# Compressed attention over one group's 64 keys, with the high and low parts stacked, and new engine orders

## The chip, the cores and the metric

One core of a Trainium2 chip runs the whole program in one launch. The metric is the device time of one execution in microseconds, as the median of several runs.

## The reference, cut to what matters

The reference is one conditioned decoder layer over 1024 tokens of width 1024: a gated feed-forward block, a mixer with two attention groups, a second feed-forward block and a final normalisation. The change lies in the first attention group, which has 8 query heads in 2 groups and three branches. Its compressed branch is this:

```
kc = compress_blocks(k_cmp, ...); vc = compress_blocks(v_cmp, ...)   # 63 blocks of each group, head size 64
s = einsum('bqgrd,bcgd->bgrqc', qb, kc) * scale
p_cmp = masked_softmax(s, cmp_end[None, :] <= t[:, None])
o_cmp = einsum('bgrqc,bcgd->bqgrd', p_cmp, vc)
o = g0 * o_cmp + g1 * o_slc + g2 * o_win
```

The other branches attend to all past keys (16 blocks of 64 are selected out of 16, so that all visible ones are taken) and to a window of 512 keys. The second attention group is a causal attention with a forgetting term, called FoX.

## The kernel before, in words

The first feed-forward block comes first, then the mixer's projections (126 products on TensorE, `mix`), then attention, the output projections and the second feed-forward block. All operands of large products are split into a high and a low part in the type fp32r, so that a product is two or three matmuls.

Attention is cut into 64 units (`A_UNITS`). A unit of the first group, kind N, is one of 2 groups g, one of 8 tiles i of 128 queries, and one of the three branches br: compressed (CMP), selected (SLC), window (WIN). It has 4 rows, one for each head of the group. The last 16 units are FoX. A row's scores are 128 queries by 128 keys times `A_LEN`; a compressed row has length 1, that is 128 keys, of which 64 belong to the group g and 64 to the other group; the mask closes those of the other group. The 244 key blocks of 128 (`A_BLOCKS`, 148 of them in the N units, 16 of these compressed) are what the value products run over.

Each unit passes through the engines so. On TensorE `scores` puts the mask in PSUM by a matmul with an identity in bf16 and then adds two matmuls for each row (high keys, low keys). On VectorE `row_max` (M) reads the scores from PSUM; on ScalarE `exp` (E) reads them too and writes the weights and their sum to SBUF; VectorE takes the reciprocal (R); on GpSimd `scale` (C) multiplies by it and by the branch's gate. TensorE transposes a block of 4 rows (T, `transpose_block`) into one of two PSUM banks; ScalarE copies that rounded as the high part (H, `high`); VectorE subtracts for the low part (L, `low_part`); TensorE multiplies both with the values (V, `values`) and accumulates over all blocks of the units of one g and i. Then the halves of a sum are added (U on ScalarE and A on VectorE), split (G, O) and stored.

Each engine does its operations in the order of a string written out in the file: `A_PE` (S scores, T, V, U for a later product), `A_DVE`, `A_ACT`, `A_POOL`. The k-th letter of a kind is its k-th item. An engine waits at an operation whose input is not there, with all behind it. T of block b waits for L of block b-2 (two PSUM banks), H of b for V of b-3 (three buffers `pt`). Scores use four PSUM banks; a pack of scores waits until the rows last in its bank have been read by E.

The masks are made once by GpSimd (`attention_masks`) at step 50 of the mixer's projections.

Of the kernel before, what the change touches and what calls it, by code (L numbers as in the profile page):

```python
# [17 lines left out]
F32 = mybir.dt.float32  # L18
# [7 lines left out]
P = 128  # L26
# [53 lines left out]
A_SUMS = [(4 * u + r, max(k, 2)) for u, r, k in A_PACKS if k > 1 or r % 2 == 0]  # L80
A_SUM_OF = [n for n, (_, k) in enumerate(A_SUMS) for _ in range(k)]
# [65 lines left out]
A_DVE = ("LMMRMLMRMRRLMMRRMLMALLRLLMMMMLMRRRMMMMRRALLMMLMLMMLMRRRRLMLRMARMLLMLRMLMLRMLLMLRMLMRLLALMMLRLMLMLRMLRMLLMLRMLMRLMALMLLMR"  # L147
         "LMRLMLRMLLMLRMLMLRLLMMRALLMLLMRLMLRMLLMLRMMRMRMMRMMRRMLMRRLMMRLMALRLMLLLLLRMLRMLMMRMRMMMRMLMLMMLMRMRRMRLLALRLALLMLMRLMLM"
         "RLALMLLMRLMLRMLMRLALMLLMLRMLLMRLMLMRLMALLMRLLMLRLLMMRLLMLMLRALMLMLLRLLMMRLLMLRMLMLRMLMARLLMLLLLRMLLMLMMRMLMLMRLRALMLMLRM"
         "LMMLLLRLLMMLMRRLMLMLRMLMMRLLMMRALMLMLRALMLLMLLMMRRLMMLMLLRRMALMLMLLRALLLLMMRLLMMLLMRRALMLMLLALRLLMLMMRLLMMLLMRRALMLMLLAL"  # L150
         "RLLMLMMRLLMMLLMRRALMLMLLMLRALLMMRLLMMLMLLMRRALMLMLLRALLLRLLLALLLLALLLLLLLLALLLLALLLLLLA")
A_ACT = ("EHEEEEHEEEEEEEHEEEEHEEEUHHGEEHHEEEHEEEEEEEEEUHHGEHEHEEHEEEHEEEHEEUEHHGEHEHEHEHHEHEHEEEEHEHUHGHEHEHEHEHEHHEHEHEEEEHUEHEHG"
         "HEHEHEHEHHEHEHEEEEHEHHUEHHGEHHEHEHEHHEHEEEEEEEEEEEEEEEEEEEHEEEEHEEEHUEHEEHGHHHHEHEHEEHEEEEEEEEEHEEHEEHEEEEEHHUEHEGHUHEHG"
         "HEHEHEHUHEGHHEHEHEHEEEEHUHGEHHEHEHHEHEHEHUEHHGEHEHEEEHEHHEHHEHUHEHEGHHHEEHHEHHEEEEHEHEHEHUEHHGHHHEHEHHEHEEHEEHEHUHEGHEHE"
         "HHHHEHHEEHEEHEHEHEHEHHUEEHEEHUGHEHEGHHEHHEEHEHEEHHUEHEGHUHHHGHEHHEHHEEHUHEEHEGHUHHHEHHGEHEHHEEUHHEEHEGHUHHHEHHGEHEHHEEUH"
         "HEEHEGHUEHHHEHHGEHHEEHEEHHUEHEGHUHHHEHHGEHHHUHHGHHUHGHHHHHHHUHHGHHUHGHHHHHUG")
# [191 lines left out]
def build(nc, aps, outs):  # L348
    ctx = ExitStack()
    with ctx:  # L350
# [157 lines left out]
        kc_hi = sb("kc_hi", [P, P], F32R)  # L508
        kc_lo = sb("kc_lo", [P, P], F32R)
# [12 lines left out]
        cmp_mask, far_edge, causal, ident_b = masks[:, 0:2048], masks[:, 2048:2176], masks[:, 2176:2304], masks[:, 2304:2432]  # L522
        edges = masks[:, 2048:2304]
# [101 lines left out]
        def s_ps(s):  # L625

            p = A_PACK_OF[s]
            u, r, k = A_PACKS[p]
            n, bank = A_LEN[u][r], A_BANK[p]
            at = bank * HALF + (s % 4 - r) * n * P + (P if n == 5 else 0)  # L630
            return at, at + n * P
# [514 lines left out]
        def _(act):  # L1146
# [480 lines left out]
            def exp(s):  # L1627

                act.wait_ge(asem["mx"], A_PACK_OF[s] + 1)
# [3 lines left out]
                act.activation(p_at(s), ps_flat[:, lo:hi], ACT.Exp, bias=negmax[:, col(s)], accum_out=rowsum[:, col(s)]).then_inc(asem["ex"], 1)  # L1633

            def high(b):

                c = a_first_row(b) * P
# [3 lines left out]
                act.copy(pt[b % 3][:, c:HALF], ps[:, 5 - b % 2, c:HALF]).then_inc(asem["ph"], 1)  # L1641
# [234 lines left out]
        def _(pool):  # L1876
# [102 lines left out]
            def attention_masks():  # L1979
# [3 lines left out]
                own(1, pool.memset(cmp_mask, NEG))  # L1983
# [112 lines left out]
        def _(dve):  # L2096
# [685 lines left out]
            def mix():  # L2782
# [3 lines left out]
                for g in range(3, M_PROD + 7):  # L2786
# [3 lines left out]
                    if g == M_PROD - 2:  # L2790
                        row_max(0)
# [903 lines left out]
```

## Time and profile before

| | us |
|---|---|
| median of 3 runs (2257.72 to 2258.95) | 2257.76 |
| the profiled execution, its own time | 2259.06 |
| its span, first to last instruction | 2257.3 |
| TensorE busy (PE) | 2218.7, 98% |
| VectorE busy (DVE) | 1560.2, 69% |
| ScalarE busy (ACT) | 1074.1, 48% |
| GpSimd busy (POOL) | 909.2, 40% |

PE is TensorE's matmuls, PEld its weight loads, which overlap matmuls. Matmuls are pipelined and overlap too, so that the cost of one in a stream is the distance between two starts, not its duration. Attention lies between 1063 and 1442 us of the span, its compressed units between 1063 and 1305 us.

### The profile page before, as it was taken

To read this page: it belongs to the slowest core of one execution; us is meant where nothing else is said; L and a number is where in the kernel's file an instruction comes from. 1 tells how busy PE (TensorE), PEld (TensorE's weight loads), DVE (VectorE), ACT (ScalarE), POOL (GpSimd) and SP (SyncE) were. 2 spreads that over 40 slices of the span, in tenths; PEclk is the share of its full clock that TensorE was granted. 3 is DMA by queue.
4 is the path that set the end of the run, shared out by engine and by line. 5 is a ranking of instruction groups with operands and counts; after the bars stand their busy time and mean duration, and the time that the engine had idled before them with its cause. 6 is when DMAs were issued, how large, how long until landed. Compare 5 with 4: busy or idle time off the path is not lost. (4 is left out here: it accounts for less than half of the span.)

```text
span 2257.3 us, 29610 instructions
## 1 busy us (share of the span) xinstructions
PE 2218.7 (98%) x10552; PEld 1821.8 (81%) x10552; DVE 1560.2 (69%) x2100; ACT 1074.1 (48%) x2026; POOL 909.2 (40%) x784
## 2 busy tenths in 40 slices
PE   7999999999999999999999999999999999999998
PEld 6888888888878888888787877788778888888887
DVE  7966767488869657632888889568786454547765
ACT  5533333333545543433989888424443333333344
POOL 0045555400123555543767555446305555530013
PEclk9999999999999999999999999999999999999999
DMA  7155665374661533454714056324223232347454
GB/s 283 70 203 213 212 220 208 133 285 154 205 224 39 173 98 143 168 187 127 196 43 113 20 124 171 110 93 159 103 74 118 98 112 95 108 156 271 142 180 159
DMA packets 152034, 338.02 MB, mean 150 GB/s; under 512 B 14224, under 2 KB 36880, under 8 KB 151888
## 3 DMA queue, kind: packets, MB, share of 16 engines
q1 hardware_dynamic: 150624, 333.57, 43.7%
q10 hardware_dynamic: 1264, 2.56, 0.5%
q8 instruction: 85, 1.39, 0.3%
q14 instruction: 61, 0.50, 0.1%
HBM read 247.28 MB, written 86.64 MB: 148 GB/s over the span
## 5 line engine op out<-in xcount | busy, mean ns | idle before, releaser
L3132 PE MATMUL ps<-r_main,r_z 128*128 128x512 f32 x1232 | 482.3, 391 | 6.5 <-DVE r_main L2176 3.6
L1928 POOL TENSOR_TENSOR r_z<-f_main,r_z 128x512 fp32r<-128x512 f32 x213 | 304.7, 1432 | 446.8 <-ACT r_z L1202 446.8
L3133 PE MATMUL ps<-r_main,r_z 128*128 128x512 f32 x1232 | 480.3, 390 | 0.0
L3134 PE MATMUL ps<-r_main,r_z 128*128 128x512 f32 x1232 | 480.0, 390 | 0.0
L1202 ACT CAST r_z<-f_main 128x512 fp32r<-128x512 f32 x254 | 155.5, 620 | 347.0 <-PE ps L3134 277.7
L3132 PEld LDWEIGHTS ps<-r_main,r_z 128*128 128x128 f32 x1232 | 231.7, 188 | 60.2 <-DVE r_main L2176 4.6
L3134 PEld LDWEIGHTS ps<-r_main,r_z 128*128 128x128 f32 x1232 | 231.8, 188 | 48.9
L3133 PEld LDWEIGHTS ps<-r_main,r_z 128*128 128x128 f32 x1232 | 231.8, 188 | 47.6 <-issue 0.2
L3278 PE MATMUL ps<-r_main 128*128 128x512 f32 x604 | 235.9, 390 | 0.2 <-DVE r_main L2428 0.2
L3280 PE MATMUL ps<-r_main 128*128 128x512 f32 x604 | 235.0, 389 | 0.0
L3279 PE MATMUL ps<-r_main 128*128 128x512 f32 x604 | 235.0, 389 | 0.0
L1964 POOL TENSOR_TENSOR r_z<-f_main,r_z 128x512 fp32r<-128x512 f32 x108 | 153.6, 1436 | 176.7 <-ACT r_z L1422 176.5
L3359 PE MATMUL ps<-r_main,r_z 128*128 128x512 f32 x504 | 198.7, 394 | 1.1 <-DVE r_main L2179 0.5
L3361 PE MATMUL ps<-r_main,r_z 128*128 128x512 f32 x504 | 196.4, 390 | 0.0
L3360 PE MATMUL ps<-r_main,r_z 128*128 128x512 f32 x504 | 196.3, 390 | 0.0
L2845 DVE TENSOR_TENSOR r_main<-ps,r_main 128x512 fp32r<-128x512 f32 x244 | 151.3, 635 | 34.8 <-ACT r_main L1641 31.5
L1641 ACT CAST r_main<-ps 128x512 fp32r<-128x512 f32 x244 | 130.7, 548 | 32.4 <-PE ps L3477 22.9
L3278 PEld LDWEIGHTS ps<-r_main 128*128 128x128 f32 x604 | 113.4, 188 | 24.5 <-issue 1.1
L3279 PEld LDWEIGHTS ps<-r_main 128*128 128x128 f32 x604 | 113.4, 188 | 24.1 <-issue 0.5
L3280 PEld LDWEIGHTS ps<-r_main 128*128 128x128 f32 x604 | 113.4, 188 | 23.4
L2830 DVE TENSOR_REDUCE negmax<-ps 128x1 f32<-128x640 f32 (+7 forms) x160 | 124.2, 790 | 7.1 <-PE ps L3464 4.8
L3359 PEld LDWEIGHTS ps<-r_main,r_z 128*128 128x128 f32 x504 | 94.6, 188 | 23.2 <-issue 2.7
(380 smaller groups left out, 4552.3 us busy)
## 6 DMA issues: line engine op xcount, KB each, us to landing
act_d<-f_main SPq DMA_DIRECT2D x154, 256.0 KB, 2.0
f_main<-act_d SPq DMA_DIRECT2D x70, 512.0 KB, 4.8
f_main<-in_ada SPq DMA_DIRECT2D x56, 512.0 KB, 5.2
f_main<-in_wg SPq DMA_DIRECT2D x20, 1024.0 KB, 5.0
f_main<-in_wu SPq DMA_DIRECT2D x20, 1024.0 KB, 5.0
f_w<-in_wo SPq DMA_DIRECT2D x40, 512.0 KB, 3.9
f_main<-in_wmix SPq DMA_DIRECT2D x18, 1024.0 KB, 5.5
f_e<-in_we SPq DMA_DIRECT2D x10, 1024.0 KB, 5.7
```

The lines of the kernel that those rows point to most:

```text
L1202: act.copy(prod_hi_t[SLOTS[g]], source_of(g)).then_inc(s["wh"], 1)
L1928: pool.tensor_tensor(prod_lo_t[slot], source_of(g), prod_hi_t[slot].bitcast(F32), ALU.subtract).then_inc(s["wl"], 1)
L1964: pool.tensor_tensor(m_lo[g % M_RING], mix_source(g), m_hi[g % M_RING].bitcast(F32), ALU.subtract).then_inc(s["wl"], 1)
L3132: pe.matmul(out, wh, hi, start=start, stop=False, skip_group_check=True)
L3133: pe.matmul(out, wh, lo, start=False, stop=False, skip_group_check=True)
L3134: return pe.matmul(out, wl, hi, start=False, stop=stop, skip_group_check=True)
L3278: pe.matmul(out, wh, hi, start=k == 0 and j in (1, 7, 2), stop=False, skip_group_check=True)
L3279: pe.matmul(out, wh, lo, start=False, stop=False, skip_group_check=True)
L3280: pe.matmul(out, wl, hi, start=False, stop=k == PAIRS - 1, skip_group_check=True).then_inc(fsem[f]["dn"], 1)
L3359: pe.matmul(out, wh, hi[:, k], start=q in (1, 7) and k == 0, stop=False, skip_group_check=True)
L3360: pe.matmul(out, wh, lo[:, k], start=False, stop=False, skip_group_check=True)
L3361: mm = pe.matmul(out, wl, hi[:, k], start=False, stop=k == 3, skip_group_check=True)
```

## The change

Scores of a compressed unit are taken over the group's own 64 keys alone. High and low keys lie side by side (`kc_st`), so that one matmul of 2 times 64 columns for each row takes the place of two of 128, and the two halves are not added in PSUM: a new VectorE operation D (`score_sum`) adds them and writes 64 sums a row to SBUF. The row maximum and the exponential read these. Weights of a compressed row are 64 columns; the transposed block has 64 partitions; its high part goes to partitions 0 to 63 and its low part to partitions 64 to 127 of the same columns. The values of a group stand twice on the partitions (`vc_twice`), and one matmul takes the place of two. The masks are smaller and made by fewer operations, and two GpSimd copies and two ScalarE copies (step 90 of the mixer's projections) make `vc_twice`. A pack of scores that follows a compressed one in its bank waits for D instead of E. All four order strings are new, for FoX too, with a D for each compressed unit but the first, whose D is in the mixer's stage.

```diff
+A_CMPS = [p for p, (u, _, _) in enumerate(A_PACKS) if A_UNITS[u][3] == CMP]
...
+def a_cols(s):
+    return HD if A_UNITS[s // 4][3] == CMP else a_len(s) * P
...
-A_PE = ("TSSTSSVSTSSVTSSVTTVTVTSSVSTSSVSSSSVVTTSSTVTSVSTSTSVTSVVVSVTTSSTVTSVTSVTSVTSVTTSVTSVTVVTSSTVTVVSTVTSVTSVTSVTSVTTSVTSVTSVTV"
-        "SVTSVTTSVVTSVTSVTSVTTSVTSVTVVTSSTTVVVSTVTSVTVTSVTSVTSVTTSSTSSSSSVSSVTSSVTSVVTVSTVTVTVTVTVTSVTSSTSSTSSSVSSVSTSVTSSTSVVVTVT"
-        "VTVTVSTSTVVTSTSVVTSVTVTSVTTSVTSVTSVTVSTVVTVSTVTSVTSVTTSVTSVTSVTVSTVTVSTVTVVTSSTTVVVSTVTSVTVSTVSTVTVTVTSSTTVVSVTTSVTSVTSVT"
-        "SVTVSVTVTVTVTVTSVTSVTTSSVTSSVSTVVTSTVSTVVTSTSSVVTVTVTVTSSVTTSVVTSSTVVTSTSSVVTVSSTTSVVSTVTVSTVTSVTVTSSVTTSSVTSVVTVSTTSVVST"
-        "VTVTVTVTVTVSSTTVSSTVVTSVTTSVVSTVTVTVTVTSTVTVSSTVSSVTVTSVTTSVVSTVTVTVTVTSTVTVSSTVSSVTVTSVTTSVVSTVTSVTTVVTSSVTVTVSTSTSVVTSV"
-        "TTSVVSTVTVTVTVTVTVTVTVTVTVUTTVVUTVTVUTVTVTVUTVTTVVUTVTVUTTVVUTVTVUTVTVTVTVVV")
-A_DVE = ("LMMRMLMRMRRLMMRRMLMALLRLLMMMMLMRRRMMMMRRALLMMLMLMMLMRRRRLMLRMARMLLMLRMLMLRMLLMLRMLMRLLALMMLRLMLMLRMLRMLLMLRMLMRLMALMLLMR"
...
+A_PE = ("SSTSSTSVTSTVSSVTTSSVTTSSSVVSTVSVSTTVSTSSSSVSTSTVVSVTTSVVSTTVSTSVTSVTSVTSVTSVSTVTSVTVTVTSSTVVVSTSVTTSVTSVTSVTSVVTTSVVTTSV"
+        "TTSVTSVVVSTTSVTSVTSVSTVTSVTTVVVTSTSVVTVSTTSVVTSTSVTSVTSVTSSSVVTSTSVTSSVTSVVTTSVSTTVSVTSVVTSSSVSSTTSSVTVTSSVSTSTVSSVTSTVV"
+        "STVTTVVTSSTVVTSVTSVVTTSVSTVTSVSTVTVSTTVSTVVTVSVTTSVTSVTVSTVTSVTSVTVTSVTSVTTVVTSSTVVTVSVTTSVVTTVSTVTSVTSVTSVTVTSVTSVTTSVT"
+        "SVVVTSVTTSVTTVVVTSVTTSVTSVSVTSSTSVTVTSVVTTSVTVTSVTTSSVVVTSTSVSTTSVVSTTSVVTSSVTVVTSTSVTSVTSVTTSVVTSVTTVVSSTTVSSTVSVTSVTVS"
+        "TVSTTVVTVTVTVTSSVTVVTSSTVTSVTTSVVSTTVVTVVTTSVTVTSSVTSSVVTTSVTTSVVSTTVVTVVTTSTVTVSSTVSSVVTTSVTVVSTTSVTSVTTVVTVSSTVTSVTSVS"
+        "TVTSVTVSTVSTTVVTVVTTVTVTVVTUTVVTTUVVTTUVTVTUVTVTUVTVTTVVUTVVTTVTVUTVTVTVTUVTVTVVV")
+A_DVE = ("DMRMMMRLMLDRRLMMRLRMLLMMRAMMRLMMRLDLRMALMMRRMMLMMLMMLRLRDMLRMLRMALMLMLMLMRLRMLRMLDRRMLLMLLMLMALMRLRMRLMLMRLMLLDRMLLMLLML"
...
+A_EARLY = [("D", 0), ("M", 0), ("M", 1), ("M", 2)]
+A_MX = {e: n + 1 for n, e in enumerate(A_EARLY + [e for e in stages(A_DVE, D=1, M=3) if e[0] in "DM"])}
...
-        kc_hi = sb("kc_hi", [P, P], F32R)
-        kc_lo = sb("kc_lo", [P, P], F32R)
+        kc_st = sb("kc_st", [P, 2, P], F32R)
+        kc_hi, kc_lo = kc_st[:, 0], kc_st[:, 1]
...
-        cmp_mask, far_edge, causal, ident_b = masks[:, 0:2048], masks[:, 2048:2176], masks[:, 2176:2304], masks[:, 2304:2432]
-        edges = masks[:, 2048:2304]
+        cmp_mask, far_edge, causal, ident_b = masks[:, 0:512], masks[:, 512:640], masks[:, 640:768], masks[:, 768:896]
+        edges = masks[:, 512:768]
+        cmp_sums = ft(19, 2)[:, 6 * P:10 * P].rearrange("p (a r c) -> p a r c", a=2, r=4)
+        vc_twice = rt(33)[:, 4 * P:6 * P].rearrange("p (g m) -> p g m", g=2)
...
+            at = A_BANK[p] * HALF + (s % 4 - r) * n * P + (P if n == 5 else 0)
+            return at, at + a_cols(s)
...
-            return p_space[seg][:, pos:pos + a_len(s) * P]
+            return p_space[seg][:, pos:pos + a_cols(s)]
+
+        def compressed_scores(u):
+
+            lo = s_ps(4 * u)[0]
+            return ps_flat[:, lo:lo + HALF].rearrange("p (r k c) -> p r k c", r=4, k=2)
+
+        def summed(u):
+
+            return cmp_sums[:, u // 3 % 2]
+
+        def compressed_block(b):
+
+            return A_UNITS[A_BLOCKS[b][0]][3] == CMP
+
+        def block_cols(b):
+
+            return slice(a_first_row(b) * P, HALF)
...
+                    if g == 90:
+                        act.wait_ge(s_mask, 8)
+                        for k in range(2):
+                            to, source = slice((1 - k) * HD, (2 - k) * HD), slice(k * HD, (k + 1) * HD)
+                            act.copy(vc_twice[to, k], vc_st[source].bitcast(F32)).then_inc(s_mask, 1)
...
-                act.wait_ge(asem["mx"], A_PACK_OF[s] + 1)
+                act.wait_ge(asem["mx"], A_MX["M", A_PACK_OF[s]])
                 if A_PLACE_FREED[s] is not None:
                     act.wait_ge(asem["tr"], A_PLACE_FREED[s] + 1)
                 lo, hi = s_ps(s)
-                act.activation(p_at(s), ps_flat[:, lo:hi], ACT.Exp, bias=negmax[:, col(s)], accum_out=rowsum[:, col(s)]).then_inc(asem["ex"], 1)
+                scored = summed(s // 4)[:, s % 4] if A_UNITS[s // 4][3] == CMP else ps_flat[:, lo:hi]
+                act.activation(p_at(s), scored, ACT.Exp, bias=negmax[:, col(s)], accum_out=rowsum[:, col(s)]).then_inc(asem["ex"], 1)
 
             def high(b):
 
-                c = a_first_row(b) * P
+                c = block_cols(b)
                 act.wait_ge(asem["tr"], b + 1)
                 if b >= 3:
                     act.wait_ge(asem["pv"], b - 2)
-                act.copy(pt[b % 3][:, c:HALF], ps[:, 5 - b % 2, c:HALF]).then_inc(asem["ph"], 1)
+                keys = HD if compressed_block(b) else P
+                act.copy(pt[b % 3][0:keys, c], ps[0:keys, 5 - b % 2, c]).then_inc(asem["ph"], 1)
...
+                pool.wait_ge(q_["cmp"], chain("cl", 1))
+                own(1, pool.memset(masks[:, 0:768], 0.0))
+                steps = cmp_mask.rearrange("p (i c) -> p i c", i=NT)
+                own(2, pool.affine_select(out=steps, in_=steps, compare_op=ALU.is_ge, fill=NEG, base=-31,
+                                          pattern=[[P, NT], [-16, HD]], channel_multiplier=1))
...
+                    own(7 + g, pool.tensor_copy(vc_twice[rows, g], vc_st[rows].bitcast(F32)))
...
+                        score_sum(0)
...
+            def score_sum(p):
+
+                rows = compressed_scores(A_PACKS[p][0])
+                dve.wait_ge(asem["sd"], p + 1)
+                dve.tensor_reduce(summed(A_PACKS[p][0]), rows.rearrange("p r k c -> p r c k"), AX.X, ALU.add).then_inc(asem["mx"], 1)
+
             def row_max(p):
 
                 u, r, k = A_PACKS[p]
                 s = 4 * u + r
                 lo, hi = s_ps(s)
+                if A_UNITS[u][3] == CMP:
+                    dve.wait_ge(asem["mx"], A_MX["D", A_CMPS.index(p)])
+                    dve.tensor_reduce(negmax[:, col(s, k)], summed(u), AX.X, ALU.max, negate=True).then_inc(asem["mx"], 1)
+                    return
...
+                if compressed_block(b):
+                    dve.tensor_tensor(pt[b % 3][HD:P, c], ps[0:HD, 5 - b % 2, c], pt[b % 3][0:HD, c].bitcast(F32), ALU.subtract).then_inc(asem["pl"], 1)
...
-                        pe.wait_ge(s_mask, 9)
+                        pe.wait_ge(s_mask, 10)
...
-                if A_BANK_FREED[p] is not None:
-                    pe.wait_ge(asem["ex"], A_BANK_FREED[p] + 1)
+                freed = A_BANK_FREED[p]
+                if freed is not None and A_UNITS[freed // 4][3] == CMP:
+                    pe.wait_ge(asem["mx"], A_MX["D", A_CMPS.index(A_PACK_OF[freed])])
+                elif freed is not None:
+                    pe.wait_ge(asem["ex"], freed + 1)
...
-                    mask = cmp_mask[:, g * T + i * P:g * T + (i + 1) * P]
-                else:
-                    mask = causal
+                    pe.matmul(compressed_scores(u)[:, :, 0], ident_b, cmp_mask[:, i * HD:(i + 1) * HD].unsqueeze(1).to_broadcast([P, 4, HD]),
+                              start=True, stop=False, skip_group_check=True)
+                    for r in range(4):
+                        mm = pe.matmul(compressed_scores(u)[:, r], q_n[g][r][:, i * P:(i + 1) * P], kc_st[:, :, g * HD:(g + 1) * HD],
+                                       start=False, stop=True, skip_group_check=True)
+                    mm.then_inc(asem["sd"], 1)
+                    return
...
+                keys = HD if compressed_block(b) else P
                 for r in range(a_first_row(b), 4):
-                    mm = pe.transpose(ps[:, 5 - b % 2, r * P:(r + 1) * P], p_at(4 * u + r)[:, j * P:(j + 1) * P], ident_f[:])
+                    mm = pe.transpose(ps[0:keys, 5 - b % 2, r * P:(r + 1) * P], p_at(4 * u + r)[:, j * P:j * P + keys], ident_f[:])
...
-                elif br == CMP:
-                    v = vc_st[:]
-                else:
+                elif br != CMP:
                     if i == 0 and br == SLC:
                         pe.wait_ge(s_nv[g], 32)
...
+                if br == CMP:
+                    mm = pe.matmul(ps[:, 6 + og % 2], vc_twice[:, g], pt[b % 3][:, 0:HALF], start=True, stop=False, skip_group_check=True)
+                    mm.then_inc(asem["pv"], 1)
+                    return
                 out = ps[:, 6 + og % 2, c:HALF]
-                pe.matmul(out, v, pt[b % 3][:, c:HALF], start=b == A_START[og], stop=False)
-                pe.matmul(out, v, pt[b % 3][:, HALF + c:T], start=False, stop=b == A_LAST[og]).then_inc(asem["pv"], 1)
+                pe.matmul(out, v, pt[b % 3][:, c:HALF], start=b == A_START[og], stop=False, skip_group_check=kind == "N")
+                pe.matmul(out, v, pt[b % 3][:, HALF + c:T], start=False, stop=b == A_LAST[og], skip_group_check=kind == "N").then_inc(asem["pv"], 1)
```

## Rows read from the trace of the kernel before

**Rows 1.** The page's first part, busy time and share of each engine.

```profile
PE 2218.7 (98%) x10552; PEld 1821.8 (81%) x10552; DVE 1560.2 (69%) x2100; ACT 1074.1 (48%) x2026; POOL 909.2 (40%) x784
```

**Rows 2.** Stretches: length, busy us (instructions) of PE PEld DVE ACT POOL, clock, DMA.

```profile
1062.90:1180.00 117.10, 112.27 (x730) 93.89 (x729) 95.80 (x172) 98.72 (x274) 71.11 (x102) 1.00 0.50 133
1180.00:1225.00 45.00, 42.25 (x273) 33.37 (x273) 36.90 (x76) 41.26 (x135) 37.11 (x61) 1.00 0.48 117
1225.00:1310.00 85.00, 84.58 (x538) 68.74 (x537) 73.58 (x122) 73.03 (x164) 44.80 (x54) 1.00 0.12 30
1310.00:1442.00 132.00, 126.39 (x786) 100.14 (x785) 109.37 (x209) 109.72 (x254) 66.73 (x76) 1.00 0.55 145
```

**Rows 3.** The same: the start, two slices of short units, one of FoX.

```profile
1062.90:1119.00 56.10, 52.23 (x340) 42.94 (x339) 42.97 (x87) 47.27 (x151) 36.07 (x61) 1.00 0.83 221
...
1080.00:1100.00 20.00, 18.53 (x116) 13.98 (x116) 17.01 (x36) 19.32 (x62) 15.86 (x28) 1.00 1.03 267
...
1200.00:1220.00 20.00, 18.33 (x114) 13.76 (x113) 16.48 (x35) 18.93 (x58) 14.84 (x24) 1.00 0.93 225
...
1360.00:1380.00 20.00, 19.00 (x122) 14.88 (x119) 18.31 (x36) 17.72 (x42) 11.77 (x15) 1.00 0.81 230
```

**Rows 4.** TensorE in order of time around one compressed unit's scores and values.

```profile
1118.98 0.38 PE L3444 MATMUL ps<-f_z 128*128 128x512 bf16 x1
1119.01 0.41 PE L3463 MATMUL ps<-kc_hi,r_main 128*128 128x128 f32 x1
1119.26 0.28 PE L3464 MATMUL ps<-kc_lo,r_main 128*128 128x128 f32 x1
...
1119.93 0.27 PE L3464 MATMUL ps<-kc_lo,r_main 128*128 128x128 f32 x1
1120.04 0.45 PE L3500 MATMUL ps<-r_main 128*128 128x512 f32 x1
...
1121.57 0.28 PE L3463 MATMUL ps<-r_main 128*128 128x256 f32 x1
1121.69 0.28 PE L3464 MATMUL ps<-r_main 128*128 128x256 f32 x1
1121.81 0.40 PE L3500 MATMUL ps<-r_main 128*128 128x512 f32 x1
...
1123.18 0.40 PE L3500 MATMUL ps<-r_main,vc_st 128*128 128x512 f32 x1
1123.42 0.39 PE L3501 MATMUL ps<-r_main,vc_st 128*128 128x512 f32 x1
```

**Rows 5.** Matmuls that read `kc_hi` (four a unit), by stretches.

```profile
1062.00:1100.00 38.00, 4.32 (x16) 3.09 (x16) 0.00 (x0) 0.00 (x0) 1.00 0.98 259
1100.00:1180.00 80.00, 5.40 (x20) 3.83 (x20) 0.00 (x0) 0.00 (x0) 1.00 0.28 74
1180.00:1225.00 45.00, 4.32 (x16) 3.11 (x16) 0.00 (x0) 0.00 (x0) 1.00 0.48 117
1225.00:1310.00 85.00, 3.24 (x12) 2.32 (x12) 0.00 (x0) 0.00 (x0) 1.00 0.12 30
```

**Rows 6.** Groups of VectorE by shape, whole span: reductions.

```profile
L2830 DVE TENSOR_REDUCE negmax<-ps 128x1 f32<-128x256 f32 x8 | 3.3, 417 | 0.2
...
L2833 DVE TENSOR_REDUCE negmax<-ps 128x2 f32<-128x512 f32 x8 | 5.5, 681 | 1.2 <-PE ps L3464 1.2
```

**Rows 7.** Groups of ScalarE by shape: exponentials, and copies from PSUM and SBUF.

```profile
L1633 ACT ACTIVATE f_main<-ps,negmax 128x640 f32<-128x640 f32 x27 | 21.6, 801 | 3.7 <-DVE negmax L2830 3.6
L1633 ACT ACTIVATE f_main<-ps,negmax 128x128 f32<-128x128 f32 x59 | 21.3, 385 | 4.4 <-DVE negmax L2833 4.2
...
L1527 ACT ACTIVATE hid_f<-hid_f 128x128 f32<-128x128 f32 x2 | 0.6, 310 | 0.0
L1525 ACT COPY hid_a<-ps 128x128 f32<-128x128 f32 x2 | 0.5, 264 | 0.0
```

**Rows 8.** The mixer's stage when GpSimd makes the masks (steps around 50).

```profile
830.00:860.00 30.00, 30.00 (x135) 24.80 (x134) 22.48 (x31) 10.03 (x19) 21.84 (x21) 1.00 0.30 106
```

**Rows 9.** Waits in 1310 to 1442 us: engine, tile, line, releaser: sum, times, longest.

```profile
PEld ps L3477 <- DVE r_main L2845: 15.3, 32, 0.9
DVE r_main L2845 <- ACT r_main L1641: 14.8, 29, 1.4
```

More of the change, by code:

```diff
@@ L152 @@
[L152 to L156, printed above, removed]
@@ L628, in s_ps @@
             u, r, k = A_PACKS[p]
-            n, bank = A_LEN[u][r], A_BANK[p]
-            at = bank * HALF + (s % 4 - r) * n * P + (P if n == 5 else 0)
-            return at, at + n * P
+            n = A_LEN[u][r]
+            at = A_BANK[p] * HALF + (s % 4 - r) * n * P + (P if n == 5 else 0)
+            return at, at + a_cols(s)
         ps_flat = ps[:].rearrange("p a b -> p (a b)")
@@ L1982, in attention_masks @@
                 pool.wait_ge(m_["pair"], 128)
-                own(1, pool.memset(cmp_mask, NEG))
-                own(2, pool.memset(masks[:, 2048:2304], 0.0))
-                for g in range(2):
-                    m = cmp_mask.rearrange("p (g i e c) -> p g i e c", g=2, i=NT, e=2)[:, g, :, g, :]
-                    own(3 + 2 * g, pool.memset(m, 0.0))
-                    own(4 + 2 * g, pool.affine_select(out=m, in_=m, compare_op=ALU.is_ge, fill=NEG, base=-31,
-                                                      pattern=[[P, NT], [-16, HD]], channel_multiplier=1))
@@ L1991, in attention_masks @@
-                own(7, pool.affine_select(out=causal, in_=causal, compare_op=ALU.is_ge, fill=NEG, base=0,
-                                          pattern=[[-1, P]], channel_multiplier=1))
-                own(8, pool.affine_select(out=far_edge, in_=far_edge, compare_op=ALU.is_ge, fill=NEG, base=-1,
-                                          pattern=[[1, P]], channel_multiplier=-1))
-                own(9, pool.tensor_copy(ident_b, ident_f[:]))
-                pool.wait_ge(q_["gt"], 1)
-                own(10, pool.affine_select(out=gate_t[:, 0, 0:24:3], in_=gate_t[:, 0, 0:24:3], compare_op=ALU.is_ge, fill=0.0, base=-31,
-                                           pattern=[[0, 8]], channel_multiplier=1))
+                pool.wait_ge(q_["cmp"], chain("cl", 1))
@@ new lines, in attention_masks @@
+                own(1, pool.memset(masks[:, 0:768], 0.0))
+                steps = cmp_mask.rearrange("p (i c) -> p i c", i=NT)
+                own(2, pool.affine_select(out=steps, in_=steps, compare_op=ALU.is_ge, fill=NEG, base=-31,
+                                          pattern=[[P, NT], [-16, HD]], channel_multiplier=1))
+                own(3, pool.affine_select(out=causal, in_=causal, compare_op=ALU.is_ge, fill=NEG, base=0,
+                                          pattern=[[-1, P]], channel_multiplier=1))
@@ new lines, in attention_masks @@
+                own(4, pool.affine_select(out=far_edge, in_=far_edge, compare_op=ALU.is_ge, fill=NEG, base=-1,
+                                          pattern=[[1, P]], channel_multiplier=-1))
+                own(5, pool.tensor_copy(ident_b, ident_f[:]))
+                pool.wait_ge(q_["gt"], 1)
+                own(6, pool.affine_select(out=gate_t[:, 0, 0:24:3], in_=gate_t[:, 0, 0:24:3], compare_op=ALU.is_ge, fill=0.0, base=-31,
+                                          pattern=[[0, 8]], channel_multiplier=1))
@@ L2001, in _ @@
+                for g in range(2):
+                    rows = slice(g * HD, (g + 1) * HD)
+                    own(7 + g, pool.tensor_copy(vc_twice[rows, g], vc_st[rows].bitcast(F32)))
             for g in range(M_PROD):
@@ L2841, in low_part @@
             def low_part(b):
[L2843 removed]
+                c = block_cols(b)
                 dve.wait_ge(asem["ph"], b + 1)
[L2845 to L2846 removed]
+                if compressed_block(b):
+                    dve.tensor_tensor(pt[b % 3][HD:P, c], ps[0:HD, 5 - b % 2, c], pt[b % 3][0:HD, c].bitcast(F32), ALU.subtract).then_inc(asem["pl"], 1)
+                else:
+                    dve.tensor_tensor(pt[b % 3][:, HALF + c.start:T], ps[:, 5 - b % 2, c], pt[b % 3][:, c].bitcast(F32),
+                                      ALU.subtract).then_inc(asem["pl"], 1)
             def o_add(og):
@@ L2856, in _ @@
             dve.wait_ge(s_mask, 10)
-            for kind, k in stages(A_DVE, M=3, R=2):
-                if kind == "M":
+            for kind, k in stages(A_DVE, D=1, M=3, R=2):
+                if kind == "D":
+                    score_sum(A_CMPS[k])
+                elif kind == "M":
                     row_max(k)
@@ L3449, in scores @@
                         q = q2 = q_n[g][r][:, i * P:(i + 1) * P]
-                        k1, k2 = (kc_hi, kc_lo) if br == CMP else (k1_n[g][br], k2_n[g][br])
-                        key0 = 0 if br == CMP else (i + 1 - n) * P
+                        k1, k2 = k1_n[g][br], k2_n[g][br]
+                        key0 = (i + 1 - n) * P
                     else:
```

23 lines of the change are left out of this document (13 added, 10 removed).

## The prediction

> **What bounds the kernel now.** I read the page's busy shares first. TensorE is busy for 98% of the span and VectorE for 69% [rows 1]; this is a kernel bound by TensorE, and a change is worth what it takes from TensorE's stream or from TensorE's waits. The change only touches attention, 1063 to 1442 us, so I read that next, by stretches [rows 2]. The reader should see four different places. In 1225 to 1310 TensorE sits idle for 0.4 of 85 us: every nanosecond of its stream counts. In 1063 to 1180 it is idle for 4.8 of 117.1, 3.9 of it before 1119 [rows 3]. In 1180 to 1225, where the second group begins with its short units, it is idle for 2.75 of 45 us. FoX has 5.6 idle of 132. The granted clock is 1.00 in all of them, the 2.4 GHz level, and TensorE was hardly ever idle before, so I expect no change of clock. The slices of short units show who limits there: ScalarE has 19.3 and 18.9 of 20 us in them [rows 3]. In FoX it is the ring T, H, L that shows: transposes wait 15.3 us for VectorE's low part, and that waits 14.8 us for ScalarE's high part [rows 9] (TensorE's weight loads run ahead, so of the 15.3 only part is lost). VectorE's share in the tight stretches is 82% (95.8 of 117.1) and 87% (73.6 of 85) [rows 2], its highest slice 92% [rows 3].
>
> **TensorE's stream, one compressed unit.** From the mask's start at 1118.98 to the start of what follows the scores at 1120.04 is 1.06 us [rows 4]. It is made of mask and first matmul, 0.28 (to 1119.26), and seven more steps of 0.111. After the change there are one mask matmul of 256 columns and four matmuls of 128. Two matmuls of 256 columns in a row start 0.12 apart, and two of 512 start 0.24 apart (1123.18 to 1123.42) [rows 4], so 256 columns fewer in the mask are worth some 0.11; the first pair is 0.17, three more steps 0.33, together 0.50 to 0.51. Saved: 0.55 us. The values go from two matmuls of 512 columns to one: 0.235 us saved, between the 0.24 just read and the 0.23 that such pairs take elsewhere. The four transposes keep their 128 moving columns but have 64 stationary columns instead of 128. A step is 0.11 us at 128 moving columns and 0.12 at 256 [rows 4], so at 128 it is not the moving columns that set it; it could be the weight load, which the change halves, or a cost of each instruction, which it doesn't. No row has 64 stationary columns. Bounds: nothing, or down to the pace of the moving columns, 0.12/2 = 0.06, which is 0.2 us for four. I take the middle, 0.1.
>
> The Trainium skill (TensorE: Matmul & The Clock Gate, section "LDWEIGHTS (loading the stationary operand)") says that a load takes its number of columns over 1.2, in ns: 107 ns for 128, 53 for 64. That fits the 0.11 of a step, and by it the four transposes would save 0.2 us a unit, 3.2 us over 16 units in place of my 1.6. No trace here shows a load of 64 columns.
>
> **Where that counts.** Scores of the 16 units fall 4, 5, 4 and 3 into 1062 to 1100, 1100 to 1180, 1180 to 1225 and 1225 to 1310 (four matmuls with `kc_hi` a unit) [rows 5]; value products follow some microseconds later, by the same order 3, 4, 3 and 6. In the second and the fourth stretch TensorE hardly waits: 8 scores by 0.55 is 4.4, and 10 value blocks by 0.235 + 0.1 is 3.35, together 7.75 us. The first unit's scores stand inside the mixer's products, where TensorE never stops: 0.55. In the short units 7 scores and 6 value blocks would be 3.85 + 2.0 = 5.85; there ScalarE or the way through C is late next, and I take half, 2.9 (bounds: none, all). Sum 11.2; if all counted, 14.15.
>
> **VectorE.** A unit gains D, a reduction that reads 512 scores a partition, and M reads 256 sums instead of 512 scores. D: the nearest row is a reduction of 512 elements, 0.68 us; M: 0.42 at 256 elements [rows 6]. So D and M are 1.10 where M was 0.68: 0.42 more, 6.7 us over 16 units. D reads its pairs 64 columns apart and writes 256 results instead of 2; no row has that. Below: 0.68. Above: twice it, 1.36, if each written result cost as much as a read one, which would be 10.9 us more in all. I take 0.68, since the same line costs the same for 2 results and for 1. In 1225 to 1310 VectorE would go from 73.6 to 74.8 us (three D) while TensorE's stretch shrinks from 85 by 3 x 0.55 + 6 x 0.335 = 3.7 to 81.3: a share of 92%, that of its highest slice now [rows 3]. It gets no cover beyond that, and I charge 1.2 us for it (bounds: 0; and 5, worked out below).
>
> **ScalarE.** 64 exponentials go from 128 to 64 columns. From 640 to 128 columns the duration falls from 801 to 385 ns, 0.81 a column, so 52 ns each [rows 7], 3.3 us in all. But they now read SBUF instead of PSUM, and the two operations on the hidden layer, both of 128 columns, are 310 ns from SBUF and 264 from PSUM [rows 7]. With those 46 ns the saving is 6 ns each, 0.4 us in all: I take nothing. So the ScalarE-bound slices don't get shorter by this.
>
> The Trainium skill (VectorE: DVE Perf Modes, section "The TRN2 errata — SBUF-src ops pay a fixed extra latency per instruction") speaks against the change here: ScalarE's fixed cost is 224 cycles from SBUF and 172 from PSUM, 43 ns more. The trace's 46 ns agrees. By columns alone ScalarE would save 3.3 us, by the rule 0.6.
>
> H and L keep their 512 columns, with half the partitions, and cost the same: a pass goes by columns. The extra two ScalarE copies (about 0.3 each, from the 310 ns row) are hidden, as ScalarE is busy for a third of the mixer's stage (10 of 30 us in this slice) [rows 8].
>
> **GpSimd and the masks.** The mask work gets smaller (a clearing of 768 in place of 2048 and more) and moves behind one more wait. It happens where GpSimd is busy for 22 of 30 us while TensorE is busy for all 30 [rows 8]; the scores that need it come 74 products later. Nothing on the path, and if that cover were gone some 2 us. `scale` for compressed rows gets shorter by some 50 ns each, which helps only in the short units.
>
> **Orders and waits.** The new D adds 0.68 us to the way from scores to exponential and M gives 0.26 back; a row's scores are issued several blocks ahead of its transposes, so this is covered except in the first two or three units of a group. What the wait for D replaces (for E of all four rows) comes earlier, in TensorE's favour. In the two strings I counted how many letters of TensorE lie between T and V of a block: the mean falls from 8.1 to 7.0 (8.7 to 7.3 in the N units), and pairs 4 or fewer apart rise from 3 to 13. That is room for H and L given away; on the other side the few very long ones (16 to 20) are gone. I take 0 for both and keep 3 us each way.
>
> **Sum.** -11.2 + 1.2 = -10.0 us. Against the profiled execution's own 2259.06 (its span 2257.3 and 1.8 around it) that is 2249.1; against the median of the runs, 2257.76, which is 1.3 below, 2247.8. I give the latter. Its own range is 2243 to 2251.
>
> **Rivals.**
> More: all of 14.15, transposes at 0.2 instead of 0.1 (1.6 more), no loss to VectorE, and the orders save some of the 13.6 us that TensorE now idles, say a fifth: about -17, 2240 to 2243. For it: idle is concentrated in a few places [rows 2], and the earlier release of the bank. Against: those places are limited by ScalarE, which saves nothing.
>
> VectorE becomes the bound: if it can't pass a share of 88% where it is now 87%, the 74.8 us of 1225 to 1310 need 85.0, and that stretch gains nothing; in 1100 to 1180, where its share is lower, the gain stays. That takes 3.7 away from 10 and leaves -6.3. If D takes 1.36 us as well, eight of them in the two tight stretches ask for 8 x 0.68 / 0.88 = 6.2 us more, and nothing is left of the gain. Between the two, nearer to the first: -5, 2253. For it: FoX, where VectorE's slices reach 92%, has TensorE at 95% [rows 3]. Against: at 87% TensorE lost just 0.5% of its time.
>
> Nothing measurable comes of it: the two together with an order that is worse by 3 to 5 us; 2254 to 2262.
>
> Slower: T and V closer together. The way T, H, L is about 0.6 + 0.6 + 0.7 = 2 us; one letter of TensorE is 379/681 = 0.56 us, so 4 letters (2.2 us) just cover it and 7 leave 1.9 us for H and L to queue behind E and M. If that queueing is as long as the room, every missing letter costs. It decides from 14.5 us on, 0.06 us for each of the 244 blocks; at 0.1 us a block it is +24 - 10 = +14, 2272; at 0.075, +8, 2266. For it: the waits of T for L and L for H in FoX. Against: the mean room of 1.9 us.
>
> **Chances.** My forecast 0.48, more 0.16, VectorE the bound 0.17, nothing 0.12, slower 0.07. About 0.2% (4.5 us) can be told from no change in this kernel. Faster is the first two and most of the third, at 2253.2 and below: 0.78; same 0.15; slower 0.07. The range 2240 to 2255 leaves out the far end of "more" and most of the last two.
>
> **What would show it.** In the profile after: a compressed unit's scores 0.5 us from the mask to the next product, and one values matmul; transposes of compressed blocks 0.06 to 0.11 apart; a D of 0.68 and an M of 0.4; exponentials of 64 columns near 380 ns; 1225 to 1310 shorter by 3 to 4 us with TensorE idle under 1 us. A TensorE that waits more for L in the N units, or D at 1 us or above, would make the forecast wrong; so would FoX differing by over 3 us, as only its order changes.

## The result and the profile after

The changed kernel takes 2237.99 us (median of 4 runs, 2237.17 to 2239.31) against 2257.74 of before beside it. The ratio is 0.9912, 95% interval 0.9900 to 0.9925: 19.8 us less (17 to 23). The forecast was 10.0 less, with 2240 as its lower end. The profiled span is 2236.3 us, 21.0 below that of before.

The page's first part after answers to [rows 1]:

```profile
PE 2201.5 (98%) x10472; PEld 1811.9 (81%) x10472; DVE 1560.2 (70%) x2116; ACT 1071.6 (48%) x2028; POOL 904.3 (40%) x782
```

Eighty matmuls are gone, 64 of the scores and 16 of the values. VectorE has just the busy time of before, though by durations D adds 10.9 us and the shorter M's give back 4.4; what made up the rest isn't shown (run 1 below, with the same operations, has 1564.7).

TensorE's instructions by line after: masks of the compressed scores, their values, and the last matmul of the other blocks' values (duration in ns least/median/most, first and last start).

```profile
L3493 PE MATMUL ps<-f_z x16: 272/283/286, 1062.9 to 1259.8; 128*128 128x256 bf16 x16
...
L3558 PE MATMUL ps<-r_main,r_z x16: 391/408/501, 1076.8 to 1287.9; 128*128 128x512 f32 x16
...
L3563 PE MATMUL ps<-r_main x228: 273/393/404, 1078.9 to 1419.5; 128*128 128x512 f32 x98, 128*128 128x256 f32 x16
```

The same work before (scores of the high keys in place of the masks):

```profile
L3463 PE MATMUL ps<-kc_hi,r_main x64: 272/277/412, 1063.1 to 1275.4; 128*128 128x128 f32 x64
...
L3501 PE MATMUL ps<-r_main x228: 272/395/403, 1080.7 to 1439.7; 128*128 128x512 f32 x98, 128*128 128x256 f32 x16
...
L3501 PE MATMUL ps<-r_main,vc_st x16: 388/394/401, 1077.4 to 1304.8; 128*128 128x512 f32 x16
```

Attention begins within 0.2 us of where it began. The last compressed value product comes 16.9 us earlier and attention's last product 20.2 us. So the time was won inside attention. The last matmul of the 148th values product, the N units' last, starts 17.5 us earlier (1325.7 before, 1308.2 after), and 2.7 us more are won behind it, in FoX. The mixer before attention and all that follows it are the same within 1 us.

Prices after, by shape: D, M of compressed units, their L.

```profile
L2863 DVE TENSOR_REDUCE f_z<-ps 128x256 f32<-128x512 f32 x16 | 10.9, 681 | 0.5 <-PE ps L3496 0.4
...
L2872 DVE TENSOR_REDUCE negmax<-f_z 128x4 f32<-128x256 f32 x16 | 6.6, 415 | 0.3
...
L2892 DVE TENSOR_TENSOR r_main<-ps,r_main 64x512 fp32r<-64x512 f32 x16 | 11.0, 685 | 1.3 <-ACT r_main L1676 0.7
```

TensorE around one compressed unit:

```profile
1077.55 0.27 PE L3493 MATMUL ps<-f_z 128*128 128x256 bf16 x1
1077.58 0.64 PE L3496 MATMUL ps<-kc_st,r_main 128*128 128x128 f32 x4
1078.19 0.60 PE L3537 MATMUL ps<-ident_f,f_main 128*64 128x128 f32 x4
1078.54 0.48 PE L3562 MATMUL ps<-r_main 128*128 128x512 f32 x1
```

Four transposes with 64 stationary columns (1078.19) take 0.35 us to the next start. Scores with their mask take 0.64 us here (1077.55 to 1078.19), and less elsewhere, as 0.52 at 1062.93 to 1063.45. D and M cost what the rows of before said, to 2 ns. TensorE's stream is 0.55 + 0.235 us shorter a unit, 12.6 in all. That leaves 7 us and more of the 19.8 which no shorter instruction of TensorE explains, and in the forecast only 11.2 of the stream was to count.

What did change is how long TensorE waits. Waits before, 1225 to 1310 us (the stretch of which I had said that every nanosecond counts), and after, 1212 to 1293, which holds about the same blocks: engine, tile, line, releaser, sum, times, longest.

```profile
DVE r_main L2845 <- ACT r_main L1641: 7.1, 17, 1.1
PEld ps L3477 <- DVE r_main L2845: 4.3, 14, 0.5
```

```profile
PEld ps L3537 <- DVE r_main L2894: 1.7, 7, 0.5
```

The weight loads of transposes (PEld) waited 14 times for a low part, 4.3 us in all, in a stretch in which TensorE had counted as busy for 84.58 of 85 us [rows 2]; after, 7 times and 1.7 us. Low parts waited 7.1 us for ScalarE's high parts, and 2.3 after.

### The profile page after: what moved, and what is told of

The parts are those of the page before. It is cut to its first block, busy times and chain, and to the rows that moved or that the text cites. A ratio compares the mean times of both kernels' runs of the same rounds, so it can differ in the third digit from the quotient of the medians.

```text
span 2236.3 us, 29463 instructions
## 1 busy us (share of the span) xinstructions
PE 2201.5 (98%) x10472; PEld 1811.9 (81%) x10472; DVE 1560.2 (70%) x2116; ACT 1071.6 (48%) x2028; POOL 904.3 (40%) x782
## 4 chain that ended last, share of the span: by engine, by line
PE 80%; DVE 12%; ACT 3%; issue 2%; DMA 1%; SPq 1%; POOL 1%; DVEq 0%; ACTq 0%; POOLq 0%
PE ps L3183 11%; PE ps L3184 11%; PE ps L3185 11%; PE ps L3331 6%; PE ps L3329 6%; PE ps L3330 6%; PE ps L3410 4%; PE ps L3412 4%; PE ps L3411 4%; PE ps L3537 3%; PE ps L3562 2%; PE ps L3141 2%; PE ps L3142 2%; PE ps L3143 2%; PE ps L3563 1%
## 5 line engine op out<-in xcount | busy, mean ns | idle before, releaser
L2894 DVE TENSOR_TENSOR r_main<-ps,r_main 128x512 fp32r<-128x512 f32 x228 | 141.3, 629 | 27.0 <-ACT r_main L1676 24.5
L1676 ACT CAST r_main<-ps 128x512 fp32r<-128x512 f32 (+1 forms) x244 | 129.1, 544 | 22.8 <-PE ps L3537 18.5
```

## The experiments

Each was timed beside the kernel before, whose median was 2257.7 (2258.1 beside runs 14 and 15). "Gain" is against it. The last column is read from each run's trace: from the first matmul of the first compressed scores to that of the 148th values product, that is, the N units. It was 262.4 us before and 245.0 after. It helps because the place where attention begins moves from execution to execution, 1061.3 to 1064.1 us, whatever the kernel; differences of 1 or 2 us between medians have to be read with that in mind.

| | median us | ratio, 95% interval | N units us |
|---|---|---|---|
| 1 edit, old orders | 2256.04 | 0.9991, 0.9982 to 1.0001 | 261.7 |
| 2 new orders, old computation | 2251.69 | 0.9971, 0.9959 to 0.9983 | 257.5 |
| 3 new orders but old from FoX on | 2239.26 | 0.9918, 0.9903 to 0.9932 | 245.3 |
| 4 D twice | 2243.79 | 0.9937, 0.9922 to 0.9952 | 249.8 |
| 5 short stream, old orders | 2254.35 | 0.9986, 0.9977 to 0.9995 | 258.9 |
| 6 short stream, new orders | 2243.48 | 0.9938, 0.9922 to 0.9955 | 250.4 |
| 7 sums in PSUM, no D | 2246.36 | 0.9949, 0.9934 to 0.9964 | 252.2 |
| 8 values twice | 2240.60 | 0.9925, 0.9910 to 0.9940 | 245.9 |
| 9 bank freed by E | 2240.71 | 0.9929, 0.9912 to 0.9945 | 248.6 |
| 10 before, half of L | 2253.10 | 0.9978, 0.9969 to 0.9987 | 257.0 |
| 11 after, half of L | 2235.49 | 0.9901, 0.9886 to 0.9916 | 242.5 |
| 12 edit, old orders, half of L | 2250.20 | 0.9967, 0.9954 to 0.9980 | 255.8 |
| 13 short stream, old orders, half of L | 2249.70 | 0.9966, 0.9953 to 0.9978 | 253.9 |
| 14 as 13, and half of H | 2241.14 | 0.9925, 0.9911 to 0.9940 | 246.2 |
| 15 as 12, and half of H | 2243.23 | 0.9933, 0.9916 to 0.9949 | 249.3 |
| 16 before, half of H | 2250.69 | 0.9967, 0.9955 to 0.9980 | 255.2 |
| 17 after, half of H | 2235.31 | 0.9900, 0.9885 to 0.9915 | 240.9 |

**1. The edit in the old orders.** The changed kernel with the four old strings; in `A_DVE` a D ahead of each compressed M.

```diff
-A_DVE = ("DMRMMMRLMLDRRLMM...   # and A_PE, A_ACT, A_POOL of the changed kernel
+A_DVE = ("LDMMRMLMRMRRLDMM...   # those of before, with D ahead of M
```

> The edited computation with the order strings of the kernel before; a D stands in VectorE's string right ahead of the M of its compressed pack. Theory A (the edit's TensorE stream gives at most 12.6 us, the other 7 us came from the new orders): 2245 to 2250, a gain of 8 to 12 us over before. Theory B (the edit alone is worth the whole 20 us, by relieving VectorE, ScalarE and the banks too, and the orders matter little): 2237 to 2241. Theory C (the edit needs its orders, since D and the shorter blocks shift every queue): no gain or a loss, 2255 or above.

**2. The new orders alone.** The kernel before with the new strings, D's taken out.

> The kernel before with the four new strings, the D letters taken out; the computation is that of before. Theory A: the new orders gain 5 to 8 us by themselves, 2250 to 2253. Theory B: within 2 us of before. Theory C (orders that fit only the new durations): slower than before, 2260 or above.

**3. The old order from FoX on.** Strings of the changed kernel up to the point, at the end of the N units, where both have issued the same items; the old ones behind it.

> The changed kernel, with the strings of the kernel before from the point on at which the first FoX units begin (both orders have issued the same items up to there). By block counts in the two traces FoX gave 3.7 us of the 20. If that is FoX's own order: 3 to 4.5 us slower than the changed kernel, 2241 to 2242.5. If it is only what the queues carry over from the N units: within 1 us of the changed kernel.

The edit by itself gains 1.7 us (an interval of 0.9982 to 1.0001, so it can hardly be told from nothing), the orders by themselves 6.0, both 19.8. They don't add up: with the new strings the edit is worth 13.7.

Run 3 is 1.3 us slower than the changed kernel, between its two expectations, but in its trace attention also began 1.6 us earlier (1061.4 against 1063.0), which hides a part. From the 145th values product, behind which TensorE's strings part, to attention's last one it takes 119.6 us against 116.5 in the changed kernel and 120.3 before. So of the 3.8 us that this stretch gained, 3.1 are its own order, and 0.7 it took over from the units before.

The trace of run 1 shows where the edit's gain went. In 1225 to 1310 us, once more:

```profile
PEld ps L3537 <- DVE r_main L2894: 6.7, 18, 0.7
```

```profile
1225.00:1310.00 85.00, 82.97 (x520) 66.19 (x518) 75.12 (x125) 71.88 (x163) 44.51 (x54) 1.00 0.12 28
```

The stream is shorter and the transposes wait more in its place, 6.7 us instead of 4.3. TensorE's last value product in attention stands at 1438.5 us, 1.2 before that of before. (This trace is of the slowest of its runs, 2257.7.)

Run 2 has another wait. In 1063 to 1290 us TensorE itself stands still for scores whose bank the exponential hasn't freed:

```profile
PE ps L3459 <- ACT f_main L1633: 4.7, 4, 1.6
```

The changed kernel has no such wait there for these scores, as D frees the bank.

**5 and 6. A shorter stream and nothing else.** Compressed units leave out the matmuls of the low keys and the low part's values matmul, in the kernel before with its own and with the new strings. No D.

```diff
-                        pe.matmul(ps_flat[:, c0:c1], q, k1[:, keys], start=c1 < hi, stop=False, skip_group_check=True)
+                        hm = pe.matmul(ps_flat[:, c0:c1], q, k1[:, keys], start=c1 < hi, stop=br == CMP, skip_group_check=True)
+                        if br == CMP:
+                            mm = hm
+                            continue
```

> The kernel before, its order strings unchanged, with work left out in compressed units: the four matmuls with the low keys and the values matmul of the low part. So TensorE's stream is 4 x 0.111 + 0.235 = 0.68 us shorter for each of 16 units (10.9 us), with no D and nothing added anywhere. The edit in the old orders gained only 1.7 us. If that is because D (and its place) ate the gain: this kernel gains 8 to 11 us, 2247 to 2250. If the old strings held the time by themselves (the ring of T, H, L, V and the waits they place), so that TensorE's stream wasn't what ran out: it gains 0 to 3 us, 2255 to 2258.

> The same with the new strings (D letters taken out), again leaving out the low keys' matmuls and the low part's values matmul. The new strings alone gave 6.0 us. If they free TensorE's stream to count: 2251.7 less 9 to 11, that is 2240 to 2243. If the two don't add up: 2246 or above. Against the changed kernel's 2238 it also shows whether D's 10.9 us of VectorE are paid for by something else (the bank that D frees early).

10.9 us less of stream are worth 3.4 in the old orders, just above the 0 to 3 expected if the strings hold the time, and 8.2 (2251.69 to 2243.48) in the new. So D isn't what ate most of the edit's gain in the old ones: without any D two thirds of it are missing too. It may have eaten some of the rest (3.4 without it, 1.7 with it).

**10 to 17. What holds the old orders.** L, H or both are done for 256 of 512 columns in the N units (in the edited kernels not in compressed blocks); the rest of the buffer keeps what it had.

```diff
+                w = HALF if A_BLOCKS[b][0] >= 6 * NT else HALF // 2
-                dve.tensor_tensor(pt[b % 3][:, HALF + c:T], ps[:, 5 - b % 2, c:HALF], pt[b % 3][:, c:HALF].bitcast(F32),
+                dve.tensor_tensor(pt[b % 3][:, HALF + c:HALF + w], ps[:, 5 - b % 2, c:w], pt[b % 3][:, c:w].bitcast(F32),
```

> The kernel before with L in the first group's units done for 256 of its 512 columns (the other half of the low part is left as it was in the buffer), 148 x 0.27 = 39.5 us of VectorE and the same off the ring of T, H, L. TensorE's stream is untouched. If TensorE's stream was the bound of the tight stretches, as I predicted from: a gain of at most 8 us, 2250 to 2258. If the ring held them: the waits in TensorE's stream up to 1310 us fall away for the most part, a gain of 12 to 25 us, 2233 to 2246.

> The same in the changed kernel, for its blocks that aren't compressed, 132 x 0.27 = 35 us of VectorE. If the new strings have taken out most of the waits for L: a gain of under 8 us, 2230 to 2238. If the ring is still as much of a bound: 12 to 25 us.

> The edit in the old strings (as in the first experiment, 2256.0) with L halved in the blocks that aren't compressed (256 of 512 columns, 132 x 0.27 = 35 us of VectorE and of the ring left out). Halving L alone gave 4.6 us in the kernel before and 2.5 in the changed one. Theory P (in the old strings TensorE's stream and the way T, H, L run out one beside the other, and taking from one alone exposes the other): together they give far more than 1.7 + 4.6 = 6.3 us, 2240 to 2246. Theory Q (what holds the old strings is something else, as ScalarE's H and E, or scores and `scale` late by the order itself): they only add up, 2250 to 2253.

> The kernel before in its own strings, with both left out: compressed units' low matmuls (10.9 us of TensorE's stream, alone worth 3.4) and half of L in the first group's units (39.5 us of VectorE, alone worth 4.6). No D, no edit. Theory P: 11 to 16 us, 2242 to 2247. Theory Q: the sum of both or less, 6 to 8 us, 2249.5 to 2252.

Of run 10's two expectations the one that the ring of T, H and L holds the time (12 to 25 us) was wrong: taking 36.4 us from VectorE (1560.2 to 1523.8 busy; I had reckoned 39.5) gains 4.6. So was theory P: stream and L together give 8.0, the sum of 3.4 and 4.6. The trace of run 13, 1225 to 1300 us, showed what was late next:

```profile
DVE r_main L2846 <- ACT r_main L1641: 12.0, 28, 1.1
...
PEld ps L3481 <- DVE r_main L2846: 1.3, 6, 0.3
```

Transposes hardly wait for L any more, but L waits for ScalarE's H, 28 times, where it had waited 17 times and 7.1 us in a slightly longer stretch before.

> The kernel with the short stream and half of L in the old strings (2249.7), with half of H left out in the first group's units too: 256 of 512 columns, 148 x 0.22 to 0.25 = 33 to 37 us of ScalarE. In it L waited for H 12.0 us in 1225 to 1300, 6.9 before. Theory R (once stream and VectorE are out of the way ScalarE's H, queued behind E, holds the old strings): 6 to 12 us faster again, 2238 to 2244. Theory S (the old strings hold the time by the order itself, whatever the durations): under 3 us, 2247 or above.

> The edit in the old strings with half of L (2250.2), and half of H left out in the blocks that aren't compressed (132 x 0.22 to 0.25 = 29 to 33 us of ScalarE). Theory R: 6 to 12 us faster again, 2238 to 2244, near the changed kernel with its full work. Theory S: 2247 or above.

> The kernel before with H in the first group's units done for 256 of its 512 columns, nothing else: 148 x 0.22 to 0.25 = 33 to 37 us of ScalarE less. On top of a shorter stream and a shorter L this gave 8.6 us. If ScalarE is what holds the old strings most, whatever the others do: 7 to 10 us, 2248 to 2251. If the three take turns and ScalarE comes last: 2 to 5 us, 2253 to 2256.

> The changed kernel with the same H halved in the blocks that aren't compressed (29 to 33 us of ScalarE). Half of L gave 2.5 us here. If the new strings left TensorE's stream as the main bound of the first group's units: under 4 us, 2234 to 2238. If ScalarE holds them too: 6 to 10 us, 2228 to 2232.

Halving H gives 8.6 and 7.0 us on top of the others, and 7.0 alone. In the old orders a shorter stream, L and H are worth 3.4, 4.6 and 7.0, 15.0 in sum; all three at once give 16.9 (run 14). So no single engine holds them. H gives most because most was taken that way: run 16 took 27.8 us from ScalarE, so a microsecond of H is worth 0.25, one of L 0.13, one of TensorE's stream 0.3. That each of them holds some of the blocks is my reading; no run goes block by block. Run 14, with 17% of VectorE's and 13% of ScalarE's busy time in the N units left out, is still 3 us slower than the changed kernel with all its work: 1.2 of it in the N units (246.2 against 245.0), most of the rest FoX's old order. In the new orders H and L are worth about 2.7 and 2.5 us (4.1 and 2.5 in the N units; the runs of 17 spread from 2233.1 to 2238.4).

**4 and 8. What is the bound in the new orders.** D twice (the first into a spare buffer), or the compressed values matmul twice.

> The changed kernel with each D done twice (the first into a spare buffer), 16 x 0.68 = 10.9 us more of VectorE. If VectorE were the bound in the N units after the change (my rival): 7 to 11 us slower, 2245 to 2249. If TensorE still is and VectorE has room: 0 to 3 us slower. My own charge of 1.2 us for the first D supposes something between.

> The changed kernel with the compressed values matmul done twice (the second overwrites the first), 16 x 0.235 = 3.8 us more of TensorE's stream. If TensorE is the bound all through: 3.5 to 4 us slower than the changed kernel, 2241.5 to 2242. If part of it is hidden in waits: 1 to 3.

10.9 us more of VectorE cost 5.8 (4.8 in the N units), between the two expectations. 3.8 us more of TensorE cost 2.6, but its runs spread from 2239.0 to 2242.5 and the N units of its trace grew by only 0.9, so this run doesn't rank the two. What ranks them is taking away: 10.9 us less of TensorE's stream gave 8.2 in the new orders (runs 2 and 6), 0.75 a microsecond, while 29.5 us less of VectorE (run 11) gave 2.5 and 23.0 less of ScalarE (run 17) 2.7, about 0.1 each. TensorE is the first bound; VectorE isn't one, but it has no room left: added work costs half its length.

**7 and 9. What D does besides adding.** Sums in PSUM again, by eight matmuls of 64 columns and no D; and D kept, but a bank freed by E.

```diff
+                        for part in range(2):
+                            mm = pe.matmul(compressed_scores(u)[:, r, 0], q_n[g][r][...], kc_st[:, part, g * HD:(g + 1) * HD], ...)
```

> The changed kernel without D: high and low keys are added in PSUM again, by eight matmuls of 64 columns a unit instead of four of 128; M and E read PSUM, the bank is freed by E. VectorE has 16 x 0.68 = 10.9 us less, TensorE eight steps of 0.06 to 0.11 instead of four of 0.11, so 0 to 7.1 us more. Doubling D cost 5.8 us. If VectorE's time is worth half its length in both directions and a step is 0.11: -5.8 + 7.1, 2239 to 2241. If a 64-column step is 0.06: 2232 to 2235. If the early release of the bank matters as well: 2243 or above.

> The changed kernel, except that a bank of compressed scores is freed by E of its last row again instead of by D; all orders and operations as in the changed kernel. The kernel with sums in PSUM and no D was 8.4 us slower than the changed one, of which 7.1 us are its 64 further matmul steps of 0.111. If the early release is what makes D pay: 1 to 5 us slower, 2239 to 2243. If the bank is never what scores wait for: within 1 us of 2238.

Freeing the bank early is worth 2.7 us (3.6 in the N units). In run 9 TensorE waits for the exponentials again, as in run 2 (1062 to 1300 us):

```profile
PE ps L3516 <- ACT f_main L1667: 4.2, 4, 1.5
```

TensorE's scores in 1087.9 to 1088.9 us of run 7 show the price of 64 moving columns:

```profile
1087.93 0.28 PE L3490 MATMUL ps<-f_z 128*128 128x256 bf16 x1
1087.97 1.06 PE L3494 MATMUL ps<-kc_st,r_main 128*128 128x64 f32 x8
1088.86 0.47 PE L3560 MATMUL ps<-r_main 128*128 128x512 f32 x1
```

Mask and eight matmuls take 0.93 us against 0.5 with four: a step of 64 columns costs the 0.11 of one of 128. 64 such steps more are 7 us of stream, 5 if they count 0.75 each as above. With the 2.7 of the bank that is 8 to 10 us, and run 7 is 8.4 slower, so taking 10.9 us from VectorE gained 1.4 us there at most.

## Why the prediction was wrong

The forecast was 10.0 us, the result 19.8. Two steps failed, and the second alone is the larger part of the 9.8 us between.

**The way of reading the bound failed.** The step was "in 1225 to 1310 TensorE sits idle for 0.4 of 85 us: every nanosecond of its stream counts". Busy time counts a matmul to its modelled end: its record lasts 0.27 to 0.39 us where the next can start after 0.11 to 0.23 [rows 4], so a wait of up to 0.16 us lies under the tail of the matmul before it. The waits of weight loads had them (4.3 us for L alone), and of such waits in FoX I had said that only a part is lost, as the "weight loads run ahead"; for this stretch I had not looked at them. Distances between starts don't rest on modelled ends. As an estimate, I took for each pair of neighbouring shapes the lower quartile of its distances in the traces of before, after, run 1 and run 2 as the pace without a wait, and summed what single distances exceed it by (above 15 ns) where the second matmul is a transpose. Transposes came late by 3.0 us in 1225 to 1310 before (38 times), not 0.4, and over the N units, to the last compressed values, by 12.3 us before, 21.5 in run 1, 4.1 in run 2 and 8.7 after. So in the old orders 9 of the 12.6 us that the edit took from the stream came back as later transposes. Only 0.3 of each us taken from the stream counted there (run 5), where I had charged 1 in the tight stretches and a half in the short units.

**The orders were sized at 0, with 3 us each way.** They are worth 6.0 us alone and 18.1 with the edit in place (2256.04 to 2237.99). Counting letters between T and V misled: the mean distance fell, I took that for room given away, and TensorE's waits for L fell from 4.3 to 1.7 us. Perhaps a long distance was a sign of queues that stood rather than of room; no run tests it. The slower rival stood on this count, and nothing of it came.

**The edit's own size came within 4 us by luck.** Alone it is worth 1.7 us, with the new orders 13.7; I had 10.0 without asking which orders. I left out that D frees the bank early (named, given no price; 2.7 us in run 9). The halving for short units took off 2.9 and the charge for VectorE 1.2; no run prices these two by themselves.

**Prices.** Scores 0.55 and values 0.235 us a unit: right. D 0.68 and M 0.42: right, 681 and 415 ns. The transposes' 0.1 a unit: wrong, they gained nothing (0.35 us for four before, at 1122.28 to 1122.63, and after), so 1.6 us of the 14.15 were never there. Exponentials of 64 columns take 345 ns, not 379, so ScalarE saves 2.6 us rather than 0.4: in run 7 the same ones read PSUM in 318 ns, 27 less, where I had taken 46 (and the figure quoted beside it was 43; the 27 hold here). FoX differing by more than 3 us was named as a sign against the forecast. It differs by 2.7 us from the 148th values product on and by 3.8 from the 145th, and run 3 shows that this is mostly its own order.

**The rivals.** "More" came nearest and I gave it 0.16; that the orders recover time was right, its size (a fifth of 13.6) came from the same misread idle time, and its 1.6 us of transposes did not come. Its terms were also added wrongly: 14.15 + 1.6 + 2.7 are 18.5, that is 2239, and not "about -17", 2240 to 2243; the result, 2238, lies below both. VectorE is not the bound (run 11), though it has no room for more work (run 4).

The cause is shown as far as this: the edit needs the new orders, these make transposes wait less, and D's early release takes away a wait of scores for exponentials that the new orders would have (runs 2 and 9). Open is what feature of the new strings does it. Each of the strings of TensorE, VectorE and ScalarE waits for items in the order of the others, and none of them was put in alone, so which letters matter was not found.

## What to carry to other kernels

When engines work through written-out orders, ask for each engine what a shorter operation there is worth before costing an edit; a busy share of 98% to 100% doesn't say it, as waits hide under the tails of matmuls. Waits of the weight loads and distances between the starts of matmuls show them. Shortening one engine's work inside an order made for the old durations gives a part only; make the order anew and time the edit, the order and both. Give a new order a price of its own in the forecast, worked out from the waits that the trace shows. When a difference is small, compare a stretch between two fixed items in the traces, not only whole times: an earlier start hid about half of what FoX's order is worth.

## What was not expected of the hardware

A weight load of 64 columns is shorter and nothing comes of it. Loads for transposes after, by shape:

```profile
L3537 PEld LDWEIGHTS ps<-ident_f,f_main 128*128 128x128 f32 x462 | 55.1, 140 | 18.0 <-DVE r_main L2894 7.2 <-POOL f_main L2079 2.4 <-issue 0.4
...
L3537 PEld LDWEIGHTS ps<-ident_f,f_main 128*64 128x64 f32 x39 | 4.1, 110 | 1.1
```

The load falls from 140 to 110 ns, the step stays at 0.11 us, and so it does with 64 moving columns (run 7). So neither the moving nor the stationary columns by themselves set a step of this size; halving both at once wasn't tried. By the rule of the Trainium skill (TensorE: Matmul & The Clock Gate, "LDWEIGHTS (loading the stationary operand)"), columns over 1.2, a load takes 107 ns for 128 columns and 53 for 64. The trace shows 140 and 110, a fall of 30 ns in place of 54, and no shorter step, so the 3.2 us that I had worked out by the rule did not come.

A reduction that writes 256 results from pairs 64 columns apart costs the same 681 ns as one that writes 2 from 512 [rows 6]. A subtraction on 64 partitions whose output lies on other partitions than its inputs costs the same 685 ns as one on 128 with the output on the same.
